# An encoder layer on one core: opening reordered, Fourier half of the output projection taken chunk by chunk

## What is computed

```python
mod = silu(c) @ w_ada + b_ada            # shift1, scale1, gate1, shift2, scale2, gate2
h = rmsnorm(x, g_attn) * (1 + scale1) + shift1
u, q, k, v = split(h @ w_in)
f_out = fourier_mix(u, w_fmix)           # real part of a 2-D DFT, then a map per group
a_out = neighbourhood_attention(rmsnorm(q, g_q), rmsnorm(k, g_k), v, rpb)
mix = concat([rmsnorm(f_out, g_fout), rmsnorm(a_out, g_aout)]) @ w_o
x = x + gate1 * mix
h2 = rmsnorm(x, g_ffn) * (1 + scale2) + shift2
return x + gate2 * ((silu(h2 @ w_gate) * (h2 @ w_up)) @ w_down)
```

## Time and profile before

| what | value |
|---|---|
| median of 3 runs | 1794.22 us (1792.05 to 1794.43) |
| profiled execution, its own time | 1798.47 us |
| its span, first to last instruction | 1796.5 us |
| PE busy, share of the span | 97% |
| DVE, ACT, POOL busy | 45%, 24%, 29% |
| granted PE clock, mean | 0.99 |

### The profile page before, as it was taken

The page is one execution under the profiler, slowest core; times in us unless marked ns, Lnnn a source line. Parts: engine busy times, 40 slices in busy tenths (PEclk is TensorE's granted clock), DMA queues, the critical chain, the costliest instruction groups (busy, mean ns, idle before and its releaser), DMA issues.

```text
span 1796.5 us, 22022 instructions
## 1 busy us (share of the span) xinstructions
PE 1741.6 (97%) x8437; PEld 1387.4 (77%) x8437; DVE 804.7 (45%) x1244; ACT 431.3 (24%) x779; POOL 524.7 (29%) x435
## 2 busy tenths in 40 slices
PE   5799999999999997999999999999999999999998
PEld 2557888866768885788888888888888888888887
DVE  3513886057874427352433425261524334242525
ACT  3312332177762016211111110101021111101110
POOL 0311221077736442040221405050503123050505
PEclk9999999999999998999999999999999999999999
DMA  9381014063113101001011110111010101110113
GB/s 352 141 324 39 25 34 77 12 139 78 49 36 133 55 1 47 24 24 47 24 35 35 35 35 23 35 35 35 12 47 23 47 23 35 35 35 23 35 35 140
DMA packets 98543, 108.70 MB, mean 61 GB/s; under 512 B 19655, under 2 KB 82337, under 8 KB 95161
## 3 DMA queue, kind: packets, MB, share of 16 engines
q1 hardware_dynamic: 97401, 104.82, 18.5%
q0 software_dynamic: 1088, 3.16, 0.5%
HBM read 98.51 MB, written 9.45 MB: 60 GB/s over the span
## 4 chain that ended last, share of the span: by engine, by line
PE 77%; DVE 2%; issue 0%; ACT 0%; POOL 0%; DVEq 0%; ACTq 0%; POOLq 0%
PE banks L101 22%; PE banks L102 22%; PE banks L103 22%; PE banks L986 2%; PE banks L995 2%; PE banks L1325 2%; PE banks L1020 2%; PE banks L1004 1%; PE banks L972 1%; DVE h_hi L1681 0%; PE banks L1794 0%; DVE xn L1674 0%; DVE h_lo L1684 0%; PE banks L1308 0%; ACT t_second L1565 0%
## 5 line engine op out<-in xcount | busy, mean ns | idle before, releaser
L1748 POOL TENSOR_TENSOR x<-x,ff_scratch 128x512 f32<-128x512 f32 x198 | 263.1, 1361 | 834.7 <-DVE ff_scratch L1641 834.1
L101 PE MATMUL banks<-h_hi,wff_hi 128*128 128x512 f32 x1056 | 414.1, 392 | 10.9 <-POOL h_lo L1735 6.1
L102 PE MATMUL banks<-h_lo,wff_hi 128*128 128x512 f32 x1056 | 412.1, 390 | 0.0
L103 PE MATMUL banks<-h_hi,wff_lo 128*128 128x512 f32 x1056 | 411.9, 390 | 0.0
L1500 DVE TENSOR_TENSOR wff_lo<-wff_raw,wff_hi 128x1024 fp32r<-128x1024 f32 x66 | 81.5, 1236 | 405.3 <-ACT wff_hi L1496 405.2
L101 PEld LDWEIGHTS banks<-h_hi,wff_hi 128*128 128x128 f32 x1056 | 199.2, 189 | 52.0 <-issue 9.3
L103 PEld LDWEIGHTS banks<-h_hi,wff_lo 128*128 128x128 f32 x1056 | 199.0, 188 | 41.5
L102 PEld LDWEIGHTS banks<-h_lo,wff_hi 128*128 128x128 f32 x1056 | 199.2, 189 | 40.3
L1641 DVE TENSOR_TENSOR ff_scratch<-banks,gate 128x512 f32<-128x512 f32 x264 | 177.3, 687 | 72.0 <-PE banks L103 49.3
L103 PE MATMUL banks<-wff_hi,ff_lo 128*128 128x512 f32 x528 | 205.4, 389 | 0.0
L102 PE MATMUL banks<-wff_lo,ff_hi 128*128 128x512 f32 x528 | 205.4, 389 | 0.0
(11 more groups left out here) (169 smaller groups left out, 2106.0 us busy)
## 6 DMA issues: line engine op xcount, KB each, us to landing
ada_rest<-in_w_ada SPq DMA_DIRECT2D x16, 1024.0 KB, 8.6
wff_raw<-in_w_gate SPq DMA_DIRECT2D x22, 512.0 KB, 4.7
wff_raw<-in_w_up SPq DMA_DIRECT2D x22, 512.0 KB, 3.9
wff_raw<-in_w_down SPq DMA_DIRECT2D x22, 512.0 KB, 3.2
ada<-in_w_ada SPq DMA_DIRECT2D x8, 1024.0 KB, 13.8
win_raw<-in_w_in SPq DMA_DIRECT2D x16, 512.0 KB, 3.9
x_first<-in_x_sample SPq DMA_DIRECT2D x2, 2048.0 KB, 16.5
wo_raw<-in_w_o SPq DMA_DIRECT2D x4, 1024.0 KB, 5.0
```

Source lines behind the costliest of these rows:

```text
L101: pe.matmul(out, lhs[0], rhs[0], start=start, stop=False)
L102: pe.matmul(out, lhs[0], rhs[1], start=False, stop=False)
L103: return pe.matmul(out, lhs[1], rhs[0], start=False, stop=stop)
L1748: pool.tensor_tensor(part, part, scratch[:, n % 3], ALU.add).then_inc(d_added, 1)
```

## The change

*Opening.* The u stores move from POOL's queue to ACT's, behind each `stage_u`. Three banks instead of two serve the turns (`x_bank`, bank 7 is new). The turns of chunk 1 move into the second tile of chunk 0 and the first of chunk 1, those of chunk 2 into the second tile of chunk 1. The mod pieces come two per tile behind tiles 1 to 8 (before: tiles 3 to 10), with a table of buffers (`SLOT`). SP loads all eight first pieces of w_ada ahead of w_in. Squares of x and the splits of w_in change places with modulations and splits of h.

*Seam.* A table `SEQ` orders the mix-outs: quarters 0 and 1 as before, then for each chunk quarter 2 and quarter 3 over its four row tiles. `FIRST` is the first mix-out of each quarter (0, 12, 24, 28) and `TURN` = [34, 42] the mix-outs behind which the turns of chunk 0 and chunk 1 begin, two per mix-out. The normalised rows of chunks 0 and 1 lie in parts of h_hi and h_lo that are no longer used (`xn_early`). DVE and ACT normalise two row tiles each (before three and one). All odd low halves go to POOL (before those of chunk 0 alone). The first tiles of the feed-forward part stand in the order GATE 0, GATE 1, UP 0, GATE 2, UP 1, UP 2 (`first_tiles`), with the turns of chunk 2 between the steps of the second and third.

```diff
+    SLOT = (0, 1, 0, 1, 2, 3, 0, 1, 2, 3, 4, 0, 1, 2, 3, 4)
     def x_bank(n):
-        return ((2, 5), (2, 5), (0, 3))[n // KT][n % 2]
+        return ((2, 5, 7), (2, 5, 7), (0, 3, 7))[n // KT][n % KT % 3]
     def pieces_at(n):
-        return {3: (0, 1), 4: (2, 3), 5: (4, 5), 6: (6, 7), 7: (8, 9), 8: (10, 11), 9: (12, 13), 10: (14, 15)}.get(n, ())
+        return (2 * n - 2, 2 * n - 1) if 1 <= n <= 8 else ()
...
             load_x(0)
-            for k in range(3, 6):
+            for k in range(3, KT):
                 load_ada0(k)
             load(0, 0)
-            load_ada0(6)
-            load_ada0(7)
             load(0, 1)
...
-            def store(j, i, s, c):
-                pool.wait_ge(bank_free, 6 * j + i + 1)
-                pool.dma_start(u_scratch[(2 * j + s) * 128:(2 * j + s) * 128 + 128, CH * c:CH * c + CH],
-                               u_stage[:, i % 2]).then_inc(u_stored[i % 2], 16)
...
-            def stage_u(j, i, bank):
+            def stage_u(j, i, s, c):
                 act.wait_ge(z_summed, 6 * j + i + 1)
                 after(act, u_stored[i % 2], 16 * (3 * j + i // 2))
-                act.activation(u_stage[:, i % 2], banks[:, bank], ACT.Copy).then_inc(bank_free, 1)
+                act.activation(u_stage[:, i % 2], banks[:, 3 * s + c], ACT.Copy).then_inc(bank_free, 1)
+                act.wait_ge(bank_free, 6 * j + i + 1)
+                act.dma_start(u_scratch[(2 * j + s) * 128:(2 * j + s) * 128 + 128, CH * c:CH * c + CH],
+                              u_stage[:, i % 2]).then_inc(u_stored[i % 2], 16)
...
+            for k in range(KT):
+                if k in (0, 4):
+                    stage_u(0, 2 + k // 4, k // 4, 1)
                 modulate(2 * KT + k)
-                if k == 3:
-                    stage_u(0, 3, 4)
...
             for k in range(KT):
                 split(k)
-            square(6)
-            square(7)
+                if k in (3, 5):
+                    square(6 + k // 5)
+                if k == 4:
+                    split_lo(dve, 0, 1)
...
                 for k in range(KT):
                     last = step((w_hi, w_lo), 3 + c, 1, c, k)
-                    if c == 1 and k == 3:
-                        turn_x(2 * KT)
-                        turn_x(2 * KT + 1)
+                    if c == 0 and k >= 3:
+                        turn_x(KT + k - 3)
+                    if c == 1:
+                        turn_x(2 * KT + k)
...
+    SEQ = [(n, t) for n in range(2) for t in range(TT)] + [
+        (n, t) for c in range(NCH) for n in range(2, OS) for t in range(4 * c, 4 * c + 4)]
+    FIRST = [SEQ.index((n, 0)) for n in range(OS)]
+    TURN = [34, 42]
...
     def on_pool(n):
-        return n < KT and n % 2 == 1
+        return n % 2 == 1
...
+        square(10)
+        split_hi(act, 0, 1)
+        square(11)
+        root(2)
+        norm(2)
+        silu(act, 0, 0)
...
+            ff_tile(0, 0)
+            h_ready(1)
+            pe.wait_ge(gated, TT * OS - 2)
+            for k in range(KT):
+                ff_step(0, 1, k)
+                if k >= 2:
+                    turn(2 * KT + k - 2)
+            pe.wait_ge(w_ready, 2)
+            pe.wait_ge(gated, TT * OS)
+            for k in range(KT):
+                ff_step(1, 0, k)
+                if k < 2:
+                    turn(3 * KT - 2 + k)
```

More of the change, by code:

```diff
@@ L328, in _ @@
                 load(2, s)
-            for q in range(7, PIECES):
+            for q in range(12, PIECES):
                 load_ada(q)
@@ L1554, in norm @@
                 act.wait_ge(turned, KT * c)
-            t = 4 * c + 3
-            act.activation(xn[:, 3], x1[:, t], ACT.Copy, scale=stat[:, 1, t:t + 1]).then_inc(xn_act, 1)
+            for i in range(2, 4):
+                t = 4 * c + i
+                act.activation(xn_tile(c, i), x1[:, t].rearrange("p (b n) -> p b n", b=2), ACT.Copy,
+                               scale=stat[:, 1, t:t + 1]).then_inc(xn_act, 1)
         def modulate(n):
@@ L1691, in run_dve @@
         dve.wait_ge(gate1_in, 16)
-        for m in range(TT * OS - 4):
+        for m in range(TT * OS):
             gate_mix(m)
@@ L1699, in run_dve @@
                 mix_recip(1)
-            if m % TT == 1 and m > TT and m // TT + 1 < OS:
-                split_o(m // TT + 1)
-        norm(0)
-        for i in range(4):
-            gate_mix(TT * OS - 4 + i)
-            if i == 2:
-                split_lo(dve, 0, 0)
-            split(2 * i)
-            split(2 * i + 1)
-        norm(1)
-        for k in range(KT):
-            split(KT + k)
+            if m in (FIRST[1] + 1, FIRST[2] + 1):
+                split_o(2 + (m > FIRST[2]))
+            if m == FIRST[3]:
+                split_lo(dve, 0, 0)
+            for c, first in enumerate(TURN):
+                if m == first - 1:
+                    norm(c)
+                if first <= m < first + 4:
+                    split(KT * c + 2 * (m - first))
+                    split(KT * c + 2 * (m - first) + 1)
         norm(2)
@@ L1735, in split @@
             pool.tensor_tensor(lo, t_ring[:, n % 2], hi.bitcast(F32), ALU.subtract).then_inc(split_pool, 1)
-        for m in range(TT * OS - 4):
+        for m in range(TT * OS):
             add_mix(m)
-        for i in range(4):
-            add_mix(TT * OS - 4 + i)
-            split(2 * i + 1)
+            for c, first in enumerate(TURN):
+                if first <= m < first + 4:
+                    split(KT * c + 2 * (m - first) + 1)
+        for k in range(1, KT, 2):
+            split(2 * KT + k)
         with pool.Fori(0, PAIRS) as j:
@@ L1806, in gate_step @@
                        (h_hi[:, k, CH * c:CH * c + CH], h_lo[:, k, CH * c:CH * c + CH]), k == 0, k == KT - 1)
             if k == KT - 1:
-                last.then_inc(g_summed, 1)
-        for m in range(TT * OS - 4):
-            if m == 2 * TT - 6:
-                f_sums()
-            mix_out(m)
-        for i in range(4):
-            mix_out(TT * OS - 4 + i)
-            turn(2 * i)
-            turn(2 * i + 1)
-        for c in range(1, NCH):
-            for k in range(KT):
-                gate_step(k, c - 1)
-                turn(KT * c + k)
@@ L1823, in pair @@
         def pair(j):
             first = isinstance(j, int) and j == 0
+            if first:
+                first_tiles()
             for i, (kind, f) in enumerate(TILES[:4]):
-                w = [part[:, i % 3].rearrange("p (k n) -> p k n", n=128) for part in (w_hi, w_lo)]
+                if first and f == 0:
+                    continue
                 pe.wait_ge(w_ready, 6 * j + i + 1)
-                for c in range(2 if first and i == 0 else 0, NCH):
-                    if f == 0 and first:
-                        if kind == UP:
-                            pe.wait_ge(t_ready, NCH * KT)
-                    elif f == 0:
+                for c in range(NCH):
+                    if f == 0:
@@ L1838, in pair @@
                         pe.wait_ge(product, 6 * j + c + 1)
[L1839 to L1842 removed]
+                    ff_tile(i, c)
             pe.wait_ge(w_ready, 6 * j + 6)
@@ L1860, in pair @@
                 last.then_inc(d_summed, 1)
+        for m in range(TT * OS):
+            if m == 2 * TT - 6:
+                f_sums()
+            mix_out(m)
+            for c, first in enumerate(TURN):
+                if first <= m < first + 4:
+                    turn(KT * c + 2 * (m - first))
+                    turn(KT * c + 2 * (m - first) + 1)
         pair(0)
```

214 lines of the change are left out of this document (97 added, 117 removed).

## The result

| | before | after |
|---|---|---|
| median | 1794.26 us (1792.05 to 1794.43) | 1764.76 us (1763.52 to 1767.65) |
| ratio after / before | | 0.9841, 95% interval 0.9824 to 0.9858 |
| profiled execution, own time | 1798.47 | 1763.52 |
| its span | 1796.5 | 1761.7 |

The change is faster by 29.5 us by the medians, 28.5 by the ratio (25.5 to 31.6). I had forecast 1766, from a gain of 28.4.

A forecast was written before the change was run, and what follows sets the result against it. PE, busy 97% of the span, was the bound, losing time in waits and low clock in the opening and at the seam. Gains of 13.2 and 15.2 made 28.4, from the median 1794.22 to 1766 us, range 1757 to 1776.

The forecast's parts named there:

- the excess: Time of a stretch beyond PE's priced work: 17.2 us in the opening behind the first tile, 20.0 at the seam.
- the chain of DVE and POOL in chunk 1: Opening: two squares and four POOL subtractions in turn leave PE waiting 2.1 us before the last step, bounds 0 to 3.5.
- the stage and store ahead of modulation 20: Opening, chunk 1's second tile: stage 0.6, issue 0.5 and modulation 0.78 on ACT make PE wait about 1.6 us.
- The start: Chunk 0: loads let it start 1.6 us earlier, moved squares cost 2.4; first tile's end +0.3, between -2.4 and +2.
- the prediction's signs: Marks of being right, among them no PE wait for POOL's h over 2 us in the opening.
- The stores: Opening: moving u stores off POOL's queue takes away PE's 3.5 us wait; each issue costs ACT 0.5.
- The mod pieces: Opening: two per tile from the first tile on cost nothing new; loads land ahead of use by 1.6 us or more.
- The seam: From mix-out 23 to the third UP tile: 4.8 of 20.0 us remain, 15.2 gained.
- The chain of chunk 2: Seam, behind the last mix-out: load, square, split and norms take 9.2 us against PE's 7.5; PE waits 1.7.
- Rival 1: Opening's supply by DVE, POOL and ACT stays the bound: opening gives 3 us, total 1776; chance 0.12.
- rival 2: Seam's waits only move, w_o quarter or UP weights late: seam gives 6 us, total 1775; chance 0.11.
- rival 3: Opening: ScalarE is held 7.5 us at each of four stores, PE loses 30, total 1799; chance 0.05.

The follow-up runs named there:

- stage behind: Changed kernel with the fourth stage of u moved behind the last modulation of chunk 2, in place of ahead of modulation 20: 1764.26 us, ratio 0.9841.
- seam-alone kernel: Changed kernel with the whole opening function of before put back, so only the seam is changed: 1779.70 us, ratio 0.9928.
- squares by ACT: Changed kernel with squares 6 and 7 (chunk 1) moved from DVE to ACT, behind its last modulation of chunk 0: 1766.10 us, ratio 0.9849.
- opening alone: Kernel of before with the opening function exchanged for the change's, the seam as before: 1780.48 us, ratio 0.9928.
- refitted list: Changed kernel with the u stores back on POOL, each placed where ACT's list has staged the tile: 1764.14 us, ratio 0.9839.
- the one trace: Changed kernel with every pair of mod pieces one tile later, behind tiles 2 to 9: 1772.72 us, ratio 0.9867; the traced execution took 1773.72.
- the two new orders: Changed kernel with UP split and first silu behind chunk 2's modulations: 1766.01 us; with that split two modulations earlier, plus chunk 1 squares and fourth-stage moves: 1762.76 us.
- the only kernel with two traces: The changed kernel, run once more without edits beside three edits of it: 1765.43 us, ratio 0.9844.

## Why the prediction was right

The forecast held: a gain of 28.4 forecast, 28.5 by the ratio, won where it was looked for. That the two figures meet so closely is in part luck. Between the two traces from which the excess was taken the gain is 34.8, 6.4 more than forecast: 2.3 in the opening, 0.2 at the seam and 3.9 in the stretch that no edit touches. Set against the profiled execution the forecast was 1770.1, and 1763.52 came. Step by step:

- **The opening behind the second tile.** I let 3.7 of the excess remain; the trace has 87.95 - 84.2 = 3.75. The parts fit less well than the sum: 2.1 forecast for the chain of DVE and POOL in chunk 1, 0.38 and 0.72 in the trace, half of it; 1.6 for the stage and store ahead of modulation 20, 1.93 in the trace, at that place, where the stage behind showed the cause; and 0.7 in gaps that the list doesn't name and that I had not forecast.
- **What was in the excess.** I counted 17.2 in the profiled execution. The seam-alone kernel with the same opening has 99.39 - 84.2 = 15.2. So 2.0 of my gain belonged to that execution: 1.5 to a fall of the clock behind the wait of 1.79, 0.5 to longer waits. Of the seam's 20.0, another 1.0 did (127.9 in both other traces with the old seam). The sum should not have been set against the median with these.
- **The start.** This is the step that was mis-sized: +0.3 for the end of the first tile, between -2.4 and +2. It came 2.1 earlier (48.38, 50.46). The squares cost what I said, 2.4 (2.1 to 2.9 by the squares by ACT), but the split of w_in, moved to the same place, I had put at nothing. The wait of 2.75, which the prediction's signs excluded, comes from both. The load order gives more than my 1.6: in the ten traces with the new load order the first step comes at 34.19 to 35.91 (mean 35.3), in the four with the old at 36.43 to 38.18 (mean 37.7), 2.4 in the mean, with a spread of 1.7 in each group. This miss and the one above it cancel by chance: opening alone against seam alone gives 13.5, I had 13.2.
- **The stores.** Right in direction, and POOL's hold was the reason, as the refitted list shows. The price was too small by the clock behind the wait: 5.6 for the long wait, and 6.2 in all, not 3.5. In the sum this did no harm, because the excess already held it.
- **The mod pieces.** "Cost nothing new" was right, but the reason was half of it: two per tile from tile 1 on also cover the preparation of chunk 1, worth 2.2 in waits and, in the one trace, 2.8 in clock.
- **The seam.** 4.8 forecast to remain, 113.52 - 108.9 = 4.6 in the trace: 1.4 for the two norms (1.4 forecast), 1.4 for the first turn of chunk 2 (1.7 forecast), 0.6 in three small waits (1.7 in four forecast), the rest in gaps that the list doesn't name. The chain of chunk 2 was as I wrote it; ACT's timeline of the changed kernel, square 10, the split, square 11, the norms:

```profile
673.85 1.03 ACT L1541 ACTIVATE banks<-x 128x1024 f32<-128x1024 f32 x1 [1.81 <-POOL x L1715]
...
677.52 1.06 ACT L1499 ACTIVATE wff_hi<-wff_raw 128x1024 fp32r<-128x1024 f32 x1 [2.53 <-DMA wff_raw<-in_w_up]
678.49 1.01 ACT L1541 ACTIVATE banks<-x 128x1024 f32<-128x1024 f32 x1
...
680.20 2.19 ACT L1555 ACTIVATE xn<-x,stat 128x1024 f32<-128x1024 f32 x2 [0.25 <-DVE stat L1656]
```

ACT sits 2.53 for the load, with the last square behind it.

- **The rest of the seam.** The low half of w_o's fourth quarter, with a cover of 1.1 forecast, was never waited for. The clock stays at 1.00 there, as forecast, with no wait over 1.4 left.
- **The rivals.** Rival 1 fell with the opening alone, rival 2 with the seam alone, rival 3 with the 0.33 of an issue.

## What to carry to other kernels

A DMA issue is cheap, but a wait ahead of it in an in-order queue costs everything behind it: ask where in the list the wait stands, not which engine issues. Price a long PE wait with the clock that may fall behind it (here 2.5 behind a wait of 3.5), and take the excess of a stretch from two executions, since one may hold a fall that the next does not. When a chain ends in several waits, the gain of removing one is read from the stretch, not from the wait's length: at the seam each of the two new orders uncovered the next wait.

## What the runs showed of the hardware that I had not expected

Code that no edit touches, from the last turn of mod to mix-out 23, took 461.3 to 466.8 us. The windows show why: the granted clock falls at three places of it, in some of the traces and not in others. First some 206 to 222 us behind the last turn of mod, in before, after and the squares-by-ACT kernel (columns as above):

```profile
358.00:374.00 16.00, 14.20 (x83) 8.87 (x83) 6.13 (x26) 8.95 (x23) 12.26 (x15) 0.79 0.91 174
```

```profile
342.00:358.00 16.00, 14.11 (x104) 9.01 (x103) 7.58 (x31) 10.03 (x27) 12.71 (x15) 1.00 0.87 146
```

```profile
342.00:358.00 16.00, 14.21 (x81) 8.54 (x79) 6.74 (x26) 9.49 (x25) 12.80 (x15) 0.79 0.94 204
```

Then 386 to 402 us behind it, in after and in the stage-behind kernel:

```profile
522.00:538.00 16.00, 16.00 (x71) 12.45 (x70) 7.22 (x12) 9.95 (x13) 9.42 (x6) 0.89 0.75 294
```

```profile
520.00:536.00 16.00, 16.00 (x77) 12.30 (x76) 7.74 (x13) 10.60 (x13) 9.41 (x6) 1.00 0.71 284
```

The stretch is 461.3 with no fall (stage behind), 462.9 with one (after), 464.5 to 465.5 with two, 466.0 to 466.8 with three (the third, in before, some 450 us behind the last turn of mod). So a fall costs some 1.4 to 2.5 us, and its places are fixed. PE's instructions in this stretch are the same in all traces, and in the second pair of windows PE counts as busy for all 16 us with the fall and without. What decides it stays open, the kernel's earlier code included, since the only kernel with two traces had the same single fall in both.

That the code up to a fall does not always decide it is shown in the first tile of the opening. The changed kernel and the opening-alone kernel have the same code up to there, and the same wait for the sixth low half (2.75 and 2.62). Behind it the clock fell in the first and not in the second:

```profile
45.00:48.00 3.00, 2.96 (x7) 1.66 (x6) 2.96 (x5) 0.00 (x0) 1.27 (x1) 0.50 1.03 357
```

```profile
45.00:48.00 3.00, 2.24 (x8) 1.20 (x8) 2.96 (x5) 0.00 (x0) 1.27 (x1) 1.00 1.02 356
```

DVE and POOL do the same in both, and PE takes 2.96 us in the one for less work than it does in 2.24 in the other. Such differences are why effects of 2 us could be read from stretches and not from totals.
